# Reordering the hand-over between expert pairs, and the last scatter, in a two-layer decoder step

## The reference, cut to what matters

```python
def moe_swiglu(h, w_router, w_gate, w_up, w_down):
    logits = (h @ w_router).astype(jnp.float32)
    top_v, top_i = lax.top_k(logits, TOP_K)
    gates = jax.nn.softmax(top_v, axis=-1)
    combine = jnp.sum(jax.nn.one_hot(top_i, N_EXPERTS, dtype=jnp.float32) * gates[..., None], axis=-2)
    out = jnp.zeros_like(h)
    for e in range(N_EXPERTS):
        out = out + combine[..., e:e + 1].astype(h.dtype) * swiglu(h, w_gate[e], w_up[e], w_down[e])
    return out

y = rms_norm(x + moe_swiglu(...), norm_final)   # over 1024 features
```

## Time and profile before

| | us |
|---|---|
| median of three timed runs | 1041.53 |
| profiled execution | 1041.68 |
| its span | 1039.9 |
| start of the first expert chunk, from the span's start | 647.37 |
| start of the last pair's scatter | 1023.55 |
| start of the final root | 1031.83 |

### The profile page before, as it was taken

The page is one execution under the profiler, slowest core; times in us unless marked ns, Lnnn a source line. Parts: engine busy times, 40 slices in busy tenths (PEclk is TensorE's granted clock), DMA queues, the critical chain, the costliest instruction groups (busy, mean ns, idle before and its releaser), DMA issues.

```text
span 1039.9 us, 25081 instructions
## 1 busy us (share of the span) xinstructions
PE 1017.7 (98%) x10835; PEld 814.7 (78%) x10835; DVE 557.5 (54%) x981; ACT 385.3 (37%) x578; POOL 101.6 (10%) x120
## 2 busy tenths in 40 slices
PE   8999999999999999999999999999999999999995
PEld 7999998799999999999999787445544644554464
DVE  6999774587666655677966564214311321332044
ACT  6776361375555543448644245000100110010003
POOL 5113020020000001110321122000000000000000
PEclk9999999999999999999999999999999999999998
DMA  9546779765555644454669957999999999999996
GB/s 354 166 157 222 255 278 386 276 203 181 183 178 200 228 172 142 144 186 156 230 208 399 397 217 280 355 421 365 387 376 396 356 364 402 371 389 355 402 366 253
DMA packets 37232, 295.20 MB, mean 284 GB/s; under 512 B 4272, under 2 KB 4528, under 8 KB 8336
## 3 DMA queue, kind: packets, MB, share of 16 engines
q1 hardware_dynamic: 34928, 284.54, 72.2%
q0 software_dynamic: 2208, 9.23, 2.8%
HBM read 287.14 MB, written 6.58 MB: 282 GB/s over the span
## 4 chain that ended last, share of the span: by engine, by line
PE 93%; DVE 3%; ACT 2%; issue 1%; DMA 1%; SPq 0%; DVEq 0%; ACTq 0%
PE ps L2092 33%; PE ps L1650 16%; PE ps L1651 16%; PE ps L1652 16%; PE ps L1930 1%; PE ps L1896 1%; PE ps L1916 1%; PE ps L2118 1%; PE ps L1870 1%; PE ps L2104 1%; ACT whi L649 1%; PE ps L1795 1%; DMA raw<-dense_in_dram 1%; DVE wlo L1036 1%; PE ps L1771 0%
## 5 line engine op out<-in xcount | busy, mean ns | idle before, releaser
L1036 DVE TENSOR_TENSOR wlo<-raw,whi 128x1024 fp32r<-128x1024 f32 (+1 forms) x180 | 238.4, 1342 | 84.8 <-ACT whi L649 78.9
L1650 PE MATMUL ps<-a_hi,whi 128*128 128x264 f32 x928 | 266.4, 287 | 3.0 <-DVE a_lo L1076 2.3
L1651 PE MATMUL ps<-a_lo,whi 128*128 128x264 f32 x928 | 263.7, 284 | 0.0
L1652 PE MATMUL ps<-a_hi,wlo 128*128 128x264 f32 x928 | 263.6, 284 | 0.0
L649 ACT ACTIVATE whi<-raw 128x1024 fp32r<-128x1024 f32 (+1 forms) x179 | 191.7, 1083 | 133.3 <-PE ps L1652 124.9
L1650 PEld LDWEIGHTS ps<-a_hi,whi 128*128 128x128 f32 x928 | 175.5, 189 | 5.0 <-issue 2.9
L1651 PEld LDWEIGHTS ps<-a_lo,whi 128*128 128x128 f32 x928 | 175.6, 189 | 0.3
L1652 PEld LDWEIGHTS ps<-a_hi,wlo 128*128 128x128 f32 x928 | 174.7, 188 | 0.0
L2092 PE MATMUL ps<-raw,xg 128*32 128x352 f32 x1536 | 116.6, 460 | 3.6 <-ACT xg L964 3.1
L2092 PE MATMUL ps<-wide,xg 128*32 128x352 f32 x1536 | 115.1, 459 | 0.0
L2092 PEld LDWEIGHTS ps<-raw,xg 128*32 128x32 f32 x1536 | 49.5, 110 | 64.5 <-issue 63.6
(11 more groups left out here) (317 smaller groups left out, 1560.8 us busy)
## 6 DMA issues: line engine op xcount, KB each, us to landing
raw<-dense_in_dram SPq DMA_DIRECT2D x59, 1024.0 KB, 4.9
raw<-moe_in_dram SPq DMA_DIRECT2D x36, 1408.0 KB, 8.4
wide<-moe_in_dram SPq DMA_DIRECT2D x36, 1408.0 KB, 10.2
raw<-gu_in_dram SPq DMA_DIRECT2D x22, 1024.0 KB, 4.8
raw<-moe_in_dram SPq DMA_DIRECT2D x12, 1536.0 KB, 9.3
wide<-moe_in_dram SPq DMA_DIRECT2D x12, 1536.0 KB, 8.9
raw<-cache_in_dram SPq DMA_DIRECT2D x12, 1024.0 KB, 8.5
wcache<-cache_in_dram SPq DMA_DIRECT2D x12, 1024.0 KB, 6.9
```

The source lines that it names most:

```text
L1036: dve.tensor_tensor(wlo[m % 4][:, 0:w], raw[:, k % RAWS, c:c + w], whi[m % 4][:, 0:w].bitcast(f32), ALU.subtract).then_inc(lo_done, 1)
L1650: pe.matmul(out, w_hi, m_hi_, start=first, stop=False)
L1651: pe.matmul(out, w_hi, m_lo_, start=False, stop=False)
L1652: return pe.matmul(out, w_lo, m_hi_, start=False, stop=last)
```

## The change

ScalarE copies the gathered tokens of the next pair ahead of the second expert's high part for pairs 0 to 2; for the last pair it copies them between that high part and the moved quarter's. The wait for the moved quarter becomes a step of its own. VectorE makes two of the three moves, then the low part of three quarters, then the third move. The slot products always use banks 3 and 4, the first gather banks 2, 5, 6, 7, so the wait between them goes; chunk 4 now waits for the slot copies, and chunk 0 of a round's first pair for the adds.

The last pair's scatter uses four tiles of 96 rows for each block (high and low part of each expert) in place of three of 128, so the packing copies fall away there; its banks are 0, 1, 5, 6; it waits for the second expert's low part of three quarters ahead of block 0, for the gather copies ahead of block 2, and for the last quarter's low part ahead of block 6. The root's table is loaded ahead of the squares, GpSimd adds the first four squared blocks into one, and TensorE sums five blocks, in the order 4, 0, 5, 6, 7.

```diff
-        def slot_bank(ahead):
-            return 3 if ahead else 6
-        def scatter_bank(f):
-            return 3 + f % 4
-        def gather_bank(n, g):
-            return ((4, 5, 6, 7) if isinstance(n, int) else (2, 5, 6, 7))[g]
+        def scatter_bank(f, last):
+            return (0, 1, 5, 6)[f % 4] if last else 3 + f % 4
+        def gather_bank(g):
+            return (2, 5, 6, 7)[g]
...
@@ GpSimd, after the loop over pairs
+            for j in range(2):
+                pool.wait_ge(n_sq, sq_of("fin", j + 1))
+                fold_chain(pool.tensor_tensor(sq_f[:, 2 * j], sq_f[:, 2 * j], sq_f[:, 2 * j + 1], ALU.add))
+            fold_chain.wait()
+            pool.tensor_tensor(sq_f[:, 0], sq_f[:, 0], sq_f[:, 2], ALU.add).then_inc(fin_fold, 1)
...
@@ ScalarE
                                        ACT.Copy, scale=slot_vs[0:CAP, p % 2, e:e + 1]).then_inc(y_h, 1)
+                    def y_hi_moved(e):
                         act.wait_ge(y_t, it * 2 + (e + 1))
                         act.activation(a_hi[0:CAP, 4 * e + 3, 0:DNQ], yt[0:CAP], ACT.Copy).then_inc(y_h, 1)
...
                     y_hi(0)
-                    y_hi(1)
-                    gathered(it + 1)
+                    y_hi_moved(0)
+                    if p < 3:
+                        gathered(it + 1)
+                        y_hi(1)
+                    else:
+                        y_hi(1)
+                        gathered(it + 1)
+                    y_hi_moved(1)
+            load_table(ACT.Sqrt)
             for j in range(2):
                 act.wait_ge(scat_add, rounds * 32 + (2 * j + 2))
                 square(sq_f[:, 2 * j:2 * j + 2], x[:, 2 * j:2 * j + 2])
             for k in range(4, KT):
                 act.wait_ge(scat_add, rounds * 32 + (k + 1))
                 square(sq_f[:, k], x[:, k])
-            load_table(ACT.Sqrt)
             root("fin", 1.0 / D)
...
@@ VectorE
-                    def y_moved(e):
+                    def y_move(e, a):
+                        b = y_banks(e)
+                        return dve.tensor_scalar(yt[32 * a:32 * a + 32],
+                                                 ps[96:128, b[a // 2], DNQ * (a % 2):DNQ * (a % 2) + DNQ],
+                                                 strip_v[96:128, a, e:e + 1], None, ALU.mult)
+                    def y_out(e):
                         dve.wait_ge(moe_used, it * PAIR_CHUNKS + (4 * e + 20))
                         if e:
                             dve.wait_ge(y_l, it * 4 + 2)
...
+                        y_move(e, 0)
+                        y_move(e, 1)
                         b = y_banks(e)[0]
                         dve.wait_ge(y_h, it * 4 + (2 * e + 1))
                         dve.scalar_tensor_tensor(
...
+                        y_move(e, 2).then_inc(y_t, 1)
                         dve.wait_ge(y_h, it * 4 + (2 * e + 2))
                         ins = dve.tensor_tensor(a_lo[0:CAP, 4 * e + 3, 0:DNQ], yt[0:CAP],
                                                 a_hi[0:CAP, 4 * e + 3, 0:DNQ].bitcast(f32), ALU.subtract)
-                        if e:
+                        if e and p < 3:
                             for a, dst in enumerate((a_hi[96:128, 0:4], a_lo[96:128, 0:4], a_lo[96:128, 4:8])):
                                 ins = dve.tensor_copy(dst[:, :, 0:DNQ], a_hi[32 * a:32 * a + 32, 4:8, 0:DNQ])
                         ins.then_inc(y_l, 1)
...
@@ TensorE
             gather(0)
             pe.wait_ge(comb_ready, 1)
-            pe.wait_ge(ga_cp, 4)
-            slots(False)
+            slots()
...
                         if u == 0 and p:
                             pe.wait_ge(y_l, r * 16 + (4 * p - 2))
+                        elif u == 0:
+                            pe.wait_ge(scat_add, it * 8 + 8)
                         if u < 4:
                             pe.wait_ge(ga_cp, it * 4 + (u + 1))
                         elif u == 4:
+                            pe.wait_ge(oht_cp, it * 2 + 2)
                             pe.wait_ge(scat_add, it * 8 + 8)
...
                     def scatter(it, p):
+                        last_pair = p == 3
                         turned_in = oht[:, p % 2]
-                        pe.wait_ge(ga_cp, it * 4 + 7)
-                        pe.wait_ge(y_l, it * 4 + 4)
+                        if not last_pair:
+                            pe.wait_ge(ga_cp, it * 4 + 7)
+                            pe.wait_ge(y_l, it * 4 + 4)
                         for f in range(KT):
+                            if last_pair and f in (0, 6):
+                                pe.wait_ge(y_l, it * 4 + (3 + f // 6))
+                            if last_pair and f == 2:
+                                pe.wait_ge(ga_cp, it * 4 + 7)
                             if f >= 4:
                                 pe.wait_ge(scat_add, it * 8 + (f + 5))
                             w = slice((f % 2) * 128, (f % 2) * 128 + 128)
-                            for j, (y, e) in enumerate(((a_hi, 0), (a_lo, 0), (a_lo, 1))):
-                                last = pe.matmul(ps[:, scatter_bank(f), 0:T], y_part(y, e, f // 2)[:, w],
-                                                 turned_in[:, j], start=j == 0, stop=j == 2)
+                            if last_pair:
+                                tiles, rows = ((a_hi, 0, 0), (a_lo, 0, 0), (a_hi, 1, 2), (a_lo, 1, 2)), CAP
+                            else:
+                                tiles, rows = ((a_hi, 0, 0), (a_lo, 0, 1), (a_lo, 1, 2)), 128
+                            for j, (y, e, t) in enumerate(tiles):
+                                last = pe.matmul(ps[:, scatter_bank(f, last_pair), 0:T], y_part(y, e, f // 2)[0:rows, w],
+                                                 turned_in[0:rows, t], start=j == 0, stop=j == len(tiles) - 1)
                             last.then_inc(scat_mm, 1)
...
-            for k in range(KT):
-                pe.wait_ge(n_sq, sq_of("fin", k // 2 + 1 if k < 4 else k - 1))
-                last = pe.matmul(ps[:, 2, 0:T], ones[:], sq_f[:, k], start=k == 0, stop=k == KT - 1)
+            for k in (4, 0, 5, 6, 7):
+                if k:
+                    pe.wait_ge(n_sq, sq_of("fin", k - 1))
+                else:
+                    pe.wait_ge(fin_fold, 1)
+                last = pe.matmul(ps[:, 2, 0:T], ones[:], sq_f[:, k], start=k == 4, stop=k == KT - 1)
             last.then_inc(n_ss, 1)
```

More of the change, by code:

```diff
@@ L301, in build @@
         conv_base, a_sq = sem("conv_base"), sem("lru_a_squared")
-        fin_g, gs_sum = sem("final_gain"), sem("slot_sums")
+        fin_g, gs_sum, fin_fold = sem("final_gain"), sem("slot_sums"), sem("final_squares_folded")
         s_hsam, row_seen, h_tok, s_rows, row_ready, xt_full = (sem(n) for n in (
@@ L963, in gathered @@
                     act.wait_ge(ga_mm, n * 4 + (g + 1))
-                    act.activation(xg[:, 2 * g:2 * g + 2, :], ps[:, gather_bank(n, g), 0:4 * CAP].rearrange(
+                    act.activation(xg[:, 2 * g:2 * g + 2, :], ps[:, gather_bank(g), 0:4 * CAP].rearrange(
                         "p (a c) -> p a c", a=2), ACT.Copy).then_inc(ga_cp, 1)
@@ L1530, in slot_values @@
                 for u in range(2):
-                    got = ps[0:CAP, slot_bank(rows) + u, 0:3 * SEL].rearrange("p (i c) -> p i c", c=SEL)
+                    got = ps[0:CAP, 3 + u, 0:3 * SEL].rearrange("p (i c) -> p i c", c=SEL)
                     both = got[:, :, 128:128 + 2 * E].rearrange("p i (h c) -> p i h c", c=E)
@@ L1548, in slot_values @@
                 for j in range(3):
-                    got = ps[32 * j:32 * j + 32, slot_bank(rows) + 1, 0:3 * SEL].rearrange("p (i c) -> p i c", c=SEL)
+                    got = ps[32 * j:32 * j + 32, 3 + 1, 0:3 * SEL].rearrange("p (i c) -> p i c", c=SEL)
                     dve.tensor_copy(turned_in[96:128, j, 0:SEQ].rearrange("p (i c) -> p i c", c=128), got[:, 0:2, 0:128])
@@ L1615, in y_lo, with scattered @@
                         ins.then_inc(y_l, 1)
-                    def scattered(it):
+                    def scattered(it, last):
                         for f in range(KT):
                             dve.wait_ge(scat_mm, it * 8 + (f + 1))
-                            dve.tensor_tensor(x[:, f], x[:, f], ps[:, scatter_bank(f), 0:T], ALU.add)\
+                            dve.tensor_tensor(x[:, f], x[:, f], ps[:, scatter_bank(f, last), 0:T], ALU.add)\
                                 .then_inc(scat_add, 1)
+                    slot_v, strip_v = slot_vs[:, p % 2], strip_vs[:, p % 2]
                     if p:
-                        scattered(r * 4 + (p - 1))
-                    slot_v, strip_v = slot_vs[:, p % 2], strip_vs[:, p % 2]
+                        scattered(r * 4 + (p - 1), False)
                     one_hots(it + 1)
@@ L1632, in _ @@
                     hidden_out(1)
[L1633 to L1636, removed]
+                    y_out(0)
+                    y_out(1)
+                scattered(r * 4 + 3, True)
             root_reciprocal("fin")
```

(10 more changed lines are left out.)

## The result

The changed kernel takes 1033.44 us (median of four runs) against 1041.37 for the kernel before on the same chip; the ratio is 0.9918, with a 95% interval of 0.9904 to 0.9932. The forecast was 1033.9 us, between 1032.6 and 1036.8. One of the four was disturbed (1463.59 us, at a mean granted clock of 0.654) and is left out of the ratio, which stands for a gain of 8.5 us; the median of the other three is 1032.74 us, just inside the range.

A forecast was written before the change was run, and what follows sets the result against it. The prediction took TensorE to bound the kernel, 93% of the chain, with the weight stream following it. Savings of 0.7 + 3.1 + 3.8 = 7.6 us gave a span of 1032.3 and a median of 1033.9 us, range 1032.6 to 1036.8.

The forecast's parts named there:

- Start of the loop: Slot products ahead of the first chunk: TensorE's wait for the fourth gather copy goes, 0.7 us.
- Boundaries: Three pair boundaries: chunk 0's wait of 1.05 us for the first gather copy goes each time, 3.1 us.
- The cover: At each pair boundary, VectorE's packing would still end 1.4 us ahead of the scatter that reads it.
- Rival C: Pair boundaries: the delayed high part makes packing late and stalls the scatter; slower, 1041.6 us and up; 6%.
- Rival D: Pair boundaries: the weight stream is the limit, so they give nothing; 1037.0 us; 4%.
- The end: Last pair through the root: earlier scatter at full clock, then the shortened sum, root 3.8 us earlier.
- rival A: Last scatter still runs at half clock; the end gives 2.9 us, the whole 1035 to 1035.5; 8%.
- GpSimd's adds: Folding the first four squared blocks behind the last scatter: each add takes 0.755 us.
- rival B: GpSimd's adds of squared blocks run at the dear price, in VectorE's way; 1036.4 us; 12%.
- The sum: Whole kernel: loop start, boundaries and end together save 0.7 + 3.1 + 3.8 = 7.6 us.

The follow-up runs named there:

- late_y: The changed kernel plus six idle ScalarE copies between gather copies and high part at the three pair boundaries; 1037.96 us, 0.9965 of the kernel before.
- undo_scatter: The changed kernel with its last pair scattered as before: three tiles of 128 rows, packing copies first, one wait; 1036.51 us, 0.9943 of the kernel before.
- yhi_first: The changed kernel with the second expert's high part ahead of the gather copies in all four pairs; 1033.56 us, 0.9921 of the kernel before.
- load_late: The changed kernel with the root's table loaded behind the squares again; 1033.01 us, 0.9921 of the kernel before.

## Why the prediction was right, step by step

- **Start of the loop**, 0.7 forecast, 1.4 measured: the term that was mis-sized. I counted the wait and not what stood behind it in the chain of before:

```profile
646.17 0.70 PE ps L2029 x6
646.87 0.49 issue
```

The 0.49 us of "issue" went too, and the slot products take 0.49 us in the change for 0.70.
- **Boundaries**, 3.1 forecast, 3.5 in the trace's stretch, and 3.1 of wait again when undone. The cover of 1.4 was 1.2. Rival C did not happen, but late_y shows where it would have begun. Rival D falls: no chunk waits for a DMA, and the stretch got shorter.
- **The end**, 3.8 forecast, 3.86 measured against the first trace of before, 4.7 against the second, whose scatter ran at half clock for longer (a mean of 0.51 over it, for 0.62 in the first); so some of the close fit is luck. The scatter started when it should (2.21 from the transposes, 2.3 forecast) and ran at full clock (1.00) behind a gap of 0.7 us, so rival A falls. Its 4.52 us for the 24 matmuls of before run from 1023.55 to 1028.07 in the earlier trace rows; the change's 32 took 3.99.
- **GpSimd's adds** took 0.73 us each for the first two, beside VectorE's adds, and 0.74 for the third; rival B falls.
- **The sum** was 7.6 forecast; the three lengths gained 8.8, and the ratio stands for 8.5. Of the 1.2 that were missing, 0.7 are the first term. Undone one at a time, the parts gave back 1.5, 3.5 and 4.1 us of these lengths.
- It was right in sum, less so in credit: I put the fold into the 3.8 us without asking what the sum would be without it. It was worth 0.3 of them, the table's move none. The banks, the split wait and the unpacked tiles did nearly all; undo_scatter takes back all three together, and no run tells them apart.

## What to carry to other kernels

When an engine's list holds a step that waits for a third engine, split the step at that wait before moving whole steps about: here the split alone, with the copies put in front of the waiting part, freed three boundaries (yhi_first), and this order left 3.1 us of cover for 1.2. Put what comes latest last in a sum: the same fold was worth 0.3 or 1.3 us. And price a stall together with the clock it leaves behind: 3.7 us of idling cost the end another 1.5 to 2.4.

## What the runs showed of the hardware that was not expected

The last group of the gather's matmuls started between 643.09 and 645.12 us in 14 traces whose code ahead of the gather is the same; that may be a good part of the spread of the times, but only the profiled executions show it. In 2 of the 14 the granted clock fell to 0.50 ahead of the loop although TensorE was busy all through that window (load_late: 2.00 of 2.00 us). What it did there were transposes of 128 columns, with short matmuls for the ranks; the same work ran at 1.00 in the other twelve, and no run tells the cause.
